# Block order in the up products of wide experts, and a finer return of the gate slots

## The reference

```
logits = u @ w_router + b_router;  top 4 of 32 experts, gates = softmax(top 4)
for each expert e, over the tokens that chose it (D = F = 1024, all float32):
    gt  = min(x @ w_gate[e] + b_gate[e], 7)
    up  = clip(x @ w_up[e] + b_up[e], -7, 7)
    hdn = (up + 1) * gt * sigmoid(1.702 * gt)
    y  += gate * (hdn @ w_down[e] + b_down[e])
```

## Time and profile before

| | us |
|---|---|
| median of 3 runs | 1350.43 (1349.25 to 1351.18) |
| the profiled execution | 1357.14 |
| its span, first to last instruction | 1355.3 |
| PE busy in the span | 1203.7 (89%) |
| DVE busy | 505.1 (37%) |
| ACT busy | 194.1 (14%) |

### The profile page before, as it was taken

The page is one execution under the profiler, slowest core; times in us unless marked ns, Lnnn a source line. Parts: engine busy times, 40 slices in busy tenths (PEclk is TensorE's granted clock), DMA queues, the critical chain, the costliest instruction groups (busy, mean ns, idle before and its releaser), DMA issues.

```text
span 1355.3 us, 21270 instructions
## 1 busy us (share of the span) xinstructions
PE 1203.7 (89%) x8482; PEld 566.1 (42%) x8483; DVE 505.1 (37%) x1099; ACT 194.1 (14%) x398; POOL 4.6 (0%) x28
## 2 busy tenths in 40 slices
PE   7998776998999798999889999889998988889796
PEld 5886564886333333343333343233333332332233
DVE  2899588802233232223222133321232322322232
ACT  2123222303011110011011001010111110111011
POOL 0000000000000000000000000000000000000000
PEclk9999787899599998999999999989999989999998
DMA  9543012862099999969999789999699999999994
GB/s 393 192 152 132 1 62 90 283 264 109 28 383 427 426 429 427 389 262 430 428 428 430 312 356 427 428 430 427 237 432 427 429 428 429 428 428 429 427 429 187
DMA packets 36804, 449.24 MB, mean 331 GB/s; under 512 B 5080, under 2 KB 5592, under 8 KB 10016
## 3 DMA queue, kind: packets, MB, share of 16 engines
q1 hardware_dynamic: 35152, 446.91, 79.2%
q10 hardware_dynamic: 1616, 1.82, 0.4%
HBM read 441.48 MB, written 7.24 MB: 331 GB/s over the span
## 4 chain that ended last, share of the span: by engine, by line
PE 55%; DMA 28%; DVE 11%; DVEq 3%; issue 2%; ACT 1%; SPq 0%; ACTq 0%
DMA ring<-in_w_experts 27%; PE ps L1378 25%; PE ps L1419 7%; DVE acts L673 5%; PE ps L1428 3%; DVEq L674 3%; PE ps L1262 2%; PE ps L1355 2%; PE ps L1319 2%; PE ps L1154 2%; PE ps L1388 2%; PE ps L1178 2%; PE ps L1253 1%; PE ps L1368 1%; PE ps L1232 1%
## 5 line engine op out<-in xcount | busy, mean ns | idle before, releaser
L1378 PE MATMUL ps<-ring,extra 128*64 128x512 f32 x1824 | 432.3, 620 | 12.6 <-DMA ring<-in_w_experts 12.6
L1419 PE MATMUL ps<-ring,extra 128*32 128x256 f32 x3072 | 206.4, 403 | 49.1 <-DMA ring<-in_w_experts 47.2
L1020 DVE TENSOR_TENSOR acts<-ps,acts 128x528 f32<-128x528 f32 x128 | 90.6, 708 | 422.7 <-PE ps L1428 218.5
L1378 PEld LDWEIGHTS ps<-ring,extra 128*64 128x64 f32 x1824 | 126.4, 141 | 269.1 <-issue 243.0
L1419 PEld LDWEIGHTS ps<-ring,extra 128*32 128x32 f32 x3072 | 89.5, 113 | 155.0 <-DMA ring<-in_w_experts 72.1
L673 DVE SCALAR_TENSOR_TENSOR acts<-acts,small 128x256 f32<-128x256 f32 x240 | 102.7, 479 | 5.2 <-ACT acts L439 0.7
L1178 PE MATMUL ps<-acts,ring 128*128 128x280 f32 (+1 forms) x320 | 79.1, 408 | 1.4 <-DVE acts L748 1.4
L1178 PEld LDWEIGHTS ps<-acts,ring 128*128 128x128 f32 x320 | 63.3, 200 | 15.6 <-issue 1.8
L1178 PE MATMUL ps<-acts,extra 128*128 128x280 f32 x256 | 61.0, 400 | 1.9 <-DVE acts L664 1.9
L1031 DVE TENSOR_SCALAR extra<-ps 128x512 f32<-128x512 f32 x32 | 22.0, 688 | 99.5 <-PE ps L1378 99.5
L1355 PE MATMUL ps<-acts 128*64 128x512 f32 (+1 forms) x228 | 57.5, 625 | 0.0
(11 more groups left out here) (286 smaller groups left out, 919.1 us busy)
## 6 DMA issues: line engine op xcount, KB each, us to landing
ring<-in_w_experts SPq DMA_DIRECT2D x192, 2048.0 KB, 21.2
ring<-in_w_in_t SPq DMA_DIRECT2D x5, 2048.0 KB, 20.9
extra<-in_w_in_t SPq DMA_DIRECT2D x4, 2048.0 KB, 12.7
ring<-in_state_t SPq DMA_DIRECT2D x8, 512.0 KB, 19.3
extra<-in_w_out_t SPq DMA_DIRECT2D x4, 1024.0 KB, 6.2
ring<-in_w_out_t SPq DMA_DIRECT2D x4, 1024.0 KB, 5.9
ring<-dtx_rows SPq DMA_DIRECT2D x8, 512.0 KB, 6.2
out_ssm_s_t<-ring SPq DMA_DIRECT2D x8, 512.0 KB, 5.1
```

The lines of the kernel that those rows point to most:

```text
L1020: TT(both, ps[:, 6:8, 0:TN], both, ALU.add).then_inc(ev["acc_done"], 1)
L1378: hs.append(MM(dst, src[:, o:o + HALF], piece(p)[:, k, 512 * h_:512 * (h_ + 1)], start=(fresh and kk == 0), stop=(kk == KT - 1), skip_grou ...
L1419: hs.append(MM(dst, src[:, o:o + QUAR], piece(p)[:, k, 256 * q:256 * (q + 1)], start=(fresh and kk == 0), stop=(kk == KT - 1), skip_group_ ...
```

## The change

Three edits go together.

1. In a wide expert the up products run block by block: pieces 4 to 7 for block 0, then pieces 4 to 7 for block 1. A new semaphore `up_first` rises behind block 0. `piece_used` now comes behind block 1 of pieces 4, 5 and 6; the fourth signal comes from the first product of `gather_s` (in narrow experts too).
2. DVE's `hidden` waits for `up_first` before block 0, and for the fourth `piece_used` only before block 1.
3. The gate slots go back in two pairs. A new semaphore `gate_half` lets SP load pair 0, `gate_used` pair 1. In a wide expert `gate_half` comes behind pieces 0 and 1 of block 1; in a small one behind piece 1 of the gate products; in a narrow one from the first up product (and `gate_used` from the second).

The core of the diff (the small and overflow experts' other lines only pass the list of handles on):

```
@@ sync
                 e = sp.value_load(order[0:1, bass.ds(i + 2, 1)], min_val=0, max_val=NE - 1)
-                sp.wait_ge(ev["gate_used"], i + 1)
                 for q in range(2):
+                    sp.wait_ge(ev[("gate_half", "gate_used")[q]], i + 1)
                     sp.dma_start(pair_row(q), expert_pair(e, q)).then_inc(landed[q], 16)
@@ vector
-            def hidden(n, i2):
-                v.wait_ge(ev["piece_used"], n * 8 + 4)
+            def hidden(n, k, i2):
                 for b in range(2):
+                    if b == 0:
+                        v.wait_ge(ev["up_first"], k + 1)
+                    else:
+                        v.wait_ge(ev["piece_used"], n * 8 + 4)
@@ tensor
...
                         h = MM(dst, S[0:r, j, 0:QUAR], xn[0:r, j, 256 * q:256 * (q + 1)], start=(j == 0), stop=(j == 2))
+                        if j == 0 and q == 0:
+                            h.then_inc(ev["piece_used"], 1)
...
             def up_of(n, i16):
-                if n == 2:
+                if n == 1:
+                    for p in range(4, 8):
+                        hs = piece_products(p, 0, xT, 2, False, i16)
+                        if p == 4:
+                            hs[0].then_inc(ev["gate_half"], 1)
+                            hs[1].then_inc(ev["gate_used"], 1)
+                        hs[-1].then_inc(ev["up_first" if p == 7 else "piece_used"], 1)
+                else:
                     bias(1, 64)
                     bias(3, 96)
                     for p in range(4):
-                        _, h = piece_products(p, 1, xT, 0, False, i16)
-                    h.then_inc(ev["gate_used"], 1)
-                for p in range(4, 8):
-                    for b in range(n):
-                        h0, h = piece_products(p, b, xT, 2, False, i16)
-                        if n == 1 and p == 4:
-                            h0.then_inc(ev["gate_used"], 1)
-                    h.then_inc(ev["piece_used"], 1)
+                        hs = piece_products(p, 1, xT, 0, False, i16)
+                        if p % 2:
+                            hs[-1].then_inc(ev[("gate_half", "gate_used")[p // 2]], 1)
+                    for p in range(4, 8):
+                        hs = piece_products(p, 0, xT, 2, False, i16)
+                    hs[-1].then_inc(ev["up_first"], 1)
+                    for p in range(4, 8):
+                        hs = piece_products(p, 1, xT, 2, False, i16)
+                        if p < 7:
+                            hs[-1].then_inc(ev["piece_used"], 1)
...
             def gate_s(i16, then):
                 for p in range(4):
-                    _, h = piece_products_s(p, xT, 0, True, i16)
+                    hs = piece_products_s(p, xT, 0, True, i16)
                     if p == 0:
                         bias_s(0, 64)
+                    if p == 1:
+                        hs[-1].then_inc(ev["gate_half"], 1)
```

More of the change, by code:

```diff
@@ L206, in build @@
                  "rows_zeroed rows_loaded xg_done sg_tr pick_done gp_ready sc_done gate_done g_ready hdn_ready "
-                 "y_back p_ready acc_done s_ready rank_ready sg_ready sort_mm order_ready o_list sig_ready gate_used piece_used o_tab f_ready f_out fsq_ready fss_mm frstd_ready iota_ready").split()
+                 "y_back p_ready acc_done s_ready rank_ready sg_ready sort_mm order_ready o_list sig_ready gate_used gate_half up_first piece_used o_tab f_ready f_out fsq_ready fss_mm frstd_ready iota_ready").split()
         ev = {n: sem(n) for n in names}
@@ L1054, in gates_of, with pair @@
                 return STT(Pm[:, bank, :], ps[:, 6, 0:TN], slot_id[:, slot:slot + 1], gp, ALU.is_equal, ALU.mult)
-            def pair(big, small_, then=None):
+            def pair(k, big, small_, then=None):
                 add_back(big * 4, then)
@@ L1060, in pair @@
                 choose_slots(slotp_s, big + 2, QUAR).then_inc(ev["s_ready"], 1)
-                hidden(big, big * 2)
+                hidden(big, k, big * 2)
                 v.wait_ge(ev["gp_ready"], big + 1)
@@ L1075, in pair @@
                 take_inputs(small_ * 2 + 2)
-            pair(0, 1, take_order)
+            pair(0, 0, 1, take_order)
             with v.Fori(0, NE // 2 - 1) as ii:
-                pair(ii * 2 + 2, ii * 2 + 3)
+                pair(ii + 1, ii * 2 + 2, ii * 2 + 3)
             TT(ktmp, cntf, capr, ALU.subtract)
@@ L1131, in _ @@
                         gate_in(j + NE)
-                        hidden(j + NE, j * 2 + 2 * NE)
+                        hidden(j + NE, j + NE // 2, j * 2 + 2 * NE)
                         v.wait_ge(ev["gp_ready"], j + NE + 1)
@@ L1379, in piece_products @@
                                      start=(fresh and kk == 0), stop=(kk == KT - 1), skip_group_check=True))
-                return hs[0], hs[-1]
+                return hs
             def scatter(n, m, n4):
@@ L1504, in up_of, with turn_hidden @@
                     for p in range(4):
-                        _, h = piece_products(p, 1, xT, 0, False, i16)
-                    h.then_inc(ev["gate_used"], 1)
-                for p in range(4, 8):
-                    for b in range(n):
-                        h0, h = piece_products(p, b, xT, 2, False, i16)
-                        if n == 1 and p == 4:
-                            h0.then_inc(ev["gate_used"], 1)
-                    h.then_inc(ev["piece_used"], 1)
-            def turn_hidden(n, i2):
+                        hs = piece_products(p, 1, xT, 0, False, i16)
[8 more added lines that the diff above has]
+                            hs[-1].then_inc(ev["piece_used"], 1)
+            def turn_hidden(n, i2, release=False):
                 for b in range(n):
@@ L1518, in turn_hidden @@
                         h = TR(ps[:, b, P * c:P * (c + 1)], hdn[:, 512 * b + P * c:512 * b + P * (c + 1)])
+                        if release and b == 0 and c == 0:
+                            h.then_inc(ev["piece_used"], 1)
                     h.then_inc(ev["ht_done"], 3 - n)
@@ L1526, in down_of @@
                             pe.wait_ge(ev["xg_out"], i2 + 3 + b)
-                        _, h = piece_products(p, b, hT_e, 4, True, i16)
-                    h.then_inc(ev["piece_used"], 1)
+                        hs = piece_products(p, b, hT_e, 4, True, i16)
+                    hs[-1].then_inc(ev["piece_used"], 1)
             def gate_s(i16, then):
                 for p in range(4):
-                    _, h = piece_products_s(p, xT, 0, True, i16)
+                    hs = piece_products_s(p, xT, 0, True, i16)
                     if p == 0:
                         bias_s(0, 64)
+                    if p == 1:
+                        hs[-1].then_inc(ev["gate_half"], 1)
                     if p == 3:
-                        h.then_inc(ev["gate_done"], 1)
+                        hs[-1].then_inc(ev["gate_done"], 1)
                     then(p)
@@ L1540, in up_s @@
                 for p in range(4, 8):
-                    h0, h = piece_products_s(p, xT, 2, True, i16)
+                    hs = piece_products_s(p, xT, 2, True, i16)
                     if p == 4:
-                        h0.then_inc(ev["gate_used"], 1)
+                        hs[0].then_inc(ev["gate_used"], 1)
                         bias_s(2, 96)
-                    h.then_inc(ev["piece_used"], 1)
+                    hs[-1].then_inc(ev["piece_used"], 1)
             def down_s(i2, i16):
@@ L1550, in down_s @@
                 for p in range(8, NP):
-                    _, h = piece_products_s(p, hT_e, 4, True, i16)
-                    h.then_inc(ev["piece_used"], 1)
+                    hs = piece_products_s(p, hT_e, 4, True, i16)
+                    hs[-1].then_inc(ev["piece_used"], 1)
             def former_ready(i):
```

7 lines of the change are left out of this document (3 added, 4 removed).

## The result

The changed kernel takes 1332.93 us, a median of 4 runs (1328.09 to 1338.56), against 1350.06 us (1349.25 to 1351.18). The ratio is 0.9871, 95% interval 0.985 to 0.9892: 17.1 us faster. A second set of 6 runs has 1331.42 against 1350.05, ratio 0.9857 (0.9826 to 0.9888). Forecast were 1326.9 us and a range of 1320 to 1338. The profiled execution took 1328.09 us, its span is 1326.2.

The account below looks back on a forecast made before the run. The weight stream was taken to bound the expert part, stalling at three wide experts. Gains of 7.85 us at each, 23.5 in all, taken from the 1350.43 us median, gave 1326.9 us; range 1320 to 1338.

Parts of the forecast that it names:

- What bounds the kernel: Expert part: bound by the weight stream, except at three wide-expert dips where it stalls; some 46 us in all to be had.
- The wait of DVE: Wide experts: with DVE waiting per block, block 1's transposes start at about 568.65 instead of 570.51, 1.86 us earlier.
- The clock: Wide experts' 64 down-product rows: with one short idle left, PE's clock holds, 1.4 us more gained (bounds 0 and 1.4).
- Rival B: Clock still falls behind the gather in wide experts; lead 1.86, gain 6.45 us each, 19.3 in all: 1331.1 us; chance 0.20.
- A: Everything as worked out at the three wide experts: 23.5 us gained, 1326.9 us, own range 1323 to 1330; chance 0.62.
- The slots: Gate pairs given back in another order: pair 0 behind a wide expert issued at 588.3 in place of 597.28.
- The forecast's queue at the first wide expert: Step-by-step transfer times there: stream holes of 17.1 us before the change, 9.3 after.
- The size: Stream gain of 7.85 us at each of three wide experts, 23.5 us in sum.
- the next pair 0 (588.3) and pair 1 (594.0) join without a hole: Small expert behind the first wide one: both gate pairs follow pair 5's end at 591.1 without stream loss, ending at 600.9.
- The estimates of 19 and 20 us: Total gains using documentation figures instead: 19 from about 358 GB/s HBM rate, 20 from a 0.6 us DMA first byte.
- Rival C: PE becomes the bound behind wide experts, only its 3.26 us lead counts, 9.8 in all: 1340.6 us; chance 0.10.
- Rival D: Slower: deeper transfer queue from small experts' earlier issues lowers stream rate; 3% would give +5 us, 1355; chance 0.03.

## Why the prediction was right, and what was too large

- What bounds the kernel: right. The rate outside the dips is unchanged, and all of the gain is in them.
- The wait of DVE: 1.86 us forecast, 1.94 measured; the idle that is left is 0.72 us, a little over the 0.3 to 0.6 forecast. Taking the wait per block away took 12.7 us of the median back, up to 3 of them a harm that the block order does without it, so it is shown as a cause, with the clock behind it.
- The clock: 1.40 forecast from the narrow experts' rows, 1.34 measured (15.29 to 13.95 us). PE's lead was 3.26 by the sum and 3.27 by the trace. Rival B fell by this, not by the time: the median of 1332.93 us lies outside A's own 1323 to 1330 and nearest to B's 1331.1. From the total alone one would have picked the wrong mechanism, and the time is inside the range because the range was widened for B and C.
- The slots: pair 0 behind a wide expert was forecast 9 us earlier and came 9.07 earlier. The late pair 2 costs nothing in the end, as the queue said.
- The forecast's queue at the first wide expert was wrong in two places that cancel out. It had a hole of 1.7 us before pair 0 in the kernel before, and a new one of 2.2 before pair 2 after the change. The landings show neither. The rate does dip behind pair 0's issue, to 336 and 319 GB/s from 552 to 554 and 554 to 556 us, but pair 0 lands 4.90 us behind its forerunner in the kernel before, as at the other two wide experts (4.91 and 4.90), and pair 2 lands 4.88 us behind in the changed one. That the 356 GB/s forecast for the first stretch met 357 is luck in part; the other two came to 367 and 366, not 375.
- The size: 7.85 us a wide expert forecast, 6.7 measured. The step that failed is "the next pair 0 (588.3) and pair 1 (594.0) join without a hole". I let a pair join for nothing if it was issued 1.65 us before the queue ran dry, the start-up of an idle queue read from the rate. By the landings that start-up is longer: the 49 pairs of the 14 profiles issued behind the landing of the pair ahead took 7.5 to 8.1 us, 2.6 us or more above the 4.90. At the first wide expert pair 5 landed 3.5 us earlier (46.9 us behind the stretch's start, 50.4 before) and pair 0 closed its hole of 4.6, so pair 0 landed 8.1 us earlier, as good as forecast. But pair 1, at a cover of 2.9, landed 6.35 us behind it: 1.45 lost, and 6.64 us are left. In all 9 profiles in which small experts give pair 0 back early and pair 1 from the first up product, pair 1 lost 1.0 to 1.6 us behind every wide expert; in the two with pair 1 given back early it lost 0.3 at most. The cover alone does not set the loss: pair 2 in wide experts, at 3.1 to 3.5 us, lost anything from nothing to 1.4.
- The same step made me call the cover at the narrow expert enough. It was in the first profile (0.1 us lost), with the stream 1.4 us late already; in the second it lost 0.4 and 1.2 us behind two wide experts.
- The estimates of 19 and 20 us were no rivals. The 19 rests on a rate that was never seen here, with 428 and 429 GB/s before and after. The 20 is a slip: in that sum both ends of the hole of 4.6 us follow a start-up, pair 5's and the next pair 0's, so a shorter one moves both and the hole stays 4.6.
- Rival C, PE as the bound behind the wide experts, fell: 9.8 us in all against some 20. Rival D fell: 429 GB/s from 974 to 1291, with more pairs in the queue.
- PE's waits for weights were to fall by 14 us, to 46; they fell to 53.0 in one profile and not at all in the other (59.4). The forecast took PE's own time as shorter by 9.8 us only. From the first load to the end, columns as in the earlier trace rows, the kernel before and the changed one have:

```profile
374.00:1355.30 981.30, 879.69 (x6922) 320.44 (x6918) 276.30 (x558) 109.66 (x231) 0.00 (x0) 0.96 0.95 399
366.00:1326.20 960.20, 871.48 (x6920) 322.52 (x6916) 276.13 (x558) 109.71 (x231) 0.00 (x0) 0.97 0.97 408
```

PE is busy 8.2 us less with the same products (13.3 less in the second profile of the changed kernel), and its waits for DVE's `hidden` fell from 18.0 to 13.0 us. Some of the busy time is a fall of the clock that is gone: the 8 rows at 663.77, 3.63 us, take 1.94 in the changed kernel:

```profile
649.07 1.94 PE L1381 MATMUL ps<-ring,extra 128*64 128x512 f32 x8 [0.62 <-DMA ring<-in_w_experts]
```

- The total: from the first load to the end 20.8 and 18.0 us, first and second profile of each kernel, 17.1 and 18.6 us in the medians. Differences of 2 to 3 us are within what the mixer part moves from run to run, and the part behind the third wide expert moves by 2.4 us too. That its length varies by up to 17 us over 14 profiles, I had not allowed for in the range; the time still lies inside.

## What to carry to other kernels

Where a ring holds just one unit of work, follow the queue of transfers step by step, with the time of each give-back: the end is set by the last give-back and by those behind it, and earlier holes make no difference. Compare marks that come once a turn of the loop, not single executions. A wait on the compute engine can cost more than itself: here 1.94 us of waiting carried 1.34 us of lower clock behind it. Give each slot back at the first instruction behind its last use, everywhere at once; with a single place the thin spot moved on (pair 1 given back early: 1.4 us regained there, 0.7 to 2.1 lost at the next narrow expert).

## What the runs showed of the hardware

- A 2048 KB transfer issued on an idle queue landed 7.5 to 8.1 us behind its issue (49 cases in 14 profiles), and 4.90 us behind its forerunner in a full queue.
- Issued 0.6 to 1.3 us before its forerunner's landing it came 6.5 to 7.1 us behind it (42 cases), issued 2.8 to 3.6 us before it 4.9 to 7.0 (53 cases), issued 3.6 to 4.6 us before it mostly 4.9 and up to 6.1 (94 cases).
- TensorE's clock fell behind idles of 0.85 and 1.48 us between transposes (0.63 granted in the 4.5 us around them, 64 rows 15.14 to 15.45 us in the two profiles), and behind 1.38 and 1.49 (16.44, 16.02 and 15.28 us). It did not fall behind a single idle of 0.72 us (13.95 us).
- Behind one wait of 2.26 us for weights the same 32 rows took 3.44 us in one kernel and 1.93 in another.
- The mixer part, with the same instructions, reached the first load of the loop at 357.4 to 374.4 us in 14 profiles.
